# Final norm moved inside the last down pass, and a re-ordered middle stage

## The reference

```
h = h + mlstm(rmsnorm(h)) ; h = h + swiglu(rmsnorm(h))           # layer 0 ("front", then FFN 0)
k, v = split(rmsnorm(h) @ w_kv)      ; k = rope(k)               # shared keys and values, 4 heads
q    = rope(rmsnorm(h) @ w_q)                                    # 16 query heads
o    = softmax([q k_meta | q k_window | sink]) @ [v_meta | v_window]   # window of 128, chunks of 64
h = h + o @ w_o                                                  # "middle stage"
h = h + swiglu(rmsnorm(h))                                       # layer 1 (FFN 1)
y = h * rsqrt(mean(h*h) + eps) * g_final                         # final norm
rope(x) = [x1 cos - x2 sin, x2 cos + x1 sin]
swiglu(x) = (silu(x w_g) * (x w_u)) @ w_down
```

## Time and profile before

| | |
|---|---|
| median of 3 runs | 2649.29 us |
| the profiled execution's own time | 2651.17 us |
| its span (first to last instruction) | 2649.4 us |
| mean granted TensorE clock | 0.992 of full speed |
| PE busy | 2587.5 us (98%) |
| DVE busy | 1097.2 us (41%) |
| ACT busy | 682.6 us (26%) |
| POOL busy | 628.9 us (24%) |
| DMA | 174.43 MB, 66 GB/s over the span |

### The profile page before, as it was taken

One profiled execution on the slowest core, in us unless ns is written; L12 is line 12 of the kernel. 1 busy time (PEld: TensorE's weight loads), 2 busy tenths in 40 slices (PEclk: granted clock), 3 DMA queues, 4 the chain that ended last, 5 costly groups with the idle time before them and its releaser, 6 DMA issues. The chain is left out here.

```text
span 2649.4 us, 37939 instructions
## 1 busy us (share of the span) xinstructions
PE 2587.5 (98%) x15350; PEld 2520.1 (95%) x15350; DVE 1097.2 (41%) x2306; ACT 682.6 (26%) x1513; POOL 628.9 (24%) x626
## 2 busy tenths in 40 slices
PE   8999999999999999999998998999999999999997
PEld 7989999999999999999997987899999999999997
DVE  6444455154322323333246555655233232223335
ACT  5222333042111111111125555434111111111112
POOL 2222213212122111121226232225112212211211
PEclk9999999999999999999999999999999999999999
DMA  4445564101111111111112136011111111111112
GB/s 146 147 123 155 159 176 147 57 25 56 32 48 40 41 48 40 40 40 40 48 51 50 43 79 160 17 33 48 40 40 41 48 33 48 48 41 41 40 40 80
DMA packets 251153, 174.43 MB, mean 66 GB/s; under 512 B 54392, under 2 KB 240940, under 8 KB 250948
## 3 DMA queue, kind: packets, MB, share of 16 engines
q1 hardware_dynamic: 250788, 171.96, 22.5%
q10 hardware_dynamic: 192, 0.04, 0.0%
HBM read 138.57 MB, written 35.20 MB: 66 GB/s over the span
## 5 line engine op out<-in xcount | busy, mean ns | idle before, releaser
L193 POOL TENSOR_TENSOR wl<-raw,wh 128x512 fp32r<-128x512 f32 x264 | 337.7, 1303 | 1291.8 <-ACT wh L185 1291.8
L345 PE MATMUL psum<-xh,wl 128*128 128x400 f32 (+1 forms) x1872 | 430.2, 338 | 0.0
L345 PE MATMUL psum<-xl,wh 128*128 128x400 f32 (+1 forms) x1872 | 428.5, 337 | 0.0
L345 PE MATMUL psum<-xh,wh 128*128 128x400 f32 (+1 forms) x1872 | 427.4, 336 | 0.0
L471 DVE TENSOR_TENSOR h<-h,psum 128x384 f32<-128x384 f32 (+1 forms) x528 | 265.1, 553 | 280.5 <-PE psum L365 267.1
L345 PEld LDWEIGHTS psum<-xh,wl 128*128 128x128 f32 x1872 | 336.8, 188 | 0.0
L345 PEld LDWEIGHTS psum<-xl,wh 128*128 128x128 f32 x1872 | 336.6, 188 | 0.0
L345 PEld LDWEIGHTS psum<-xh,wh 128*128 128x128 f32 x1872 | 335.9, 188 | 0.0
L2023 PE MATMUL psum<-xh,wh 128*128 128x384 f32 (+1 forms) x792 | 275.7, 348 | 5.5 <-DVE xl L2173 2.7
L2023 PE MATMUL psum<-xl,wh 128*128 128x384 f32 (+1 forms) x792 | 271.4, 343 | 0.0
L2023 PE MATMUL psum<-xh,wl 128*128 128x384 f32 (+1 forms) x792 | 270.0, 341 | 0.0
(11 more groups left out here) (249 smaller groups left out, 3687.2 us busy)
## 6 DMA issues: line engine op xcount, KB each, us to landing
raw<-in_w_gate_up SPq DMA_DIRECT2D x88, 512.0 KB, 3.8
raw<-in_w_down SPq DMA_DIRECT2D x44, 512.0 KB, 3.6
raw<-in_a_w_in SPq DMA_DIRECT2D x24, 512.0 KB, 4.7
fr_qkv<-qkv_d SPq DMA_DIRECT2D x36, 256.0 KB, 3.8
qkv_d<-fr_tmp SPq DMA_DIRECT2D x32, 192.0 KB, 2.0
hn_d<-fr_hn_turned SPq DMA_DIRECT2D x36, 128.0 KB, 3.3
fr_xin<-in_x_prompt SPq DMA_DIRECT2D x8, 512.0 KB, 5.2
fr_decode_state<-in_state_c SPq DMA_DIRECT2D x4, 1024.0 KB, 7.2
```

The lines of the kernel that those rows point to most:

```text
L193: pool.tensor_tensor(wl[:, self.slot(p), v], raw[:, self.raw_of(p), v], wh[:, self.slot(p), v].bitcast(F32), ALU.subtract).then_inc(self.w ...
L345: y = pe.matmul(psum[:, bank + c, 0:nt], w[:, k, :], x[:, k, t0:t0 + nt], start=(k == 0 and m == 0), stop=(k == KD - 1 and m == 2))
```

## The change

Final norm:

- Block `final` is gone; a class `Final` works inside the one block. ACT squares each tile of `h` as DVE adds it, POOL sums them, for each token piece. In the down pass, `between` puts PE work behind the tiles m = 2 to 7 of pieces 1 and 2: at m = 2 the token sums of the piece before (three matmuls of one column), and at each of m = 2 to 7 four transposes of it (`turn`). DVE scales the turned tiles between its adds (`after`). The third piece is turned and scaled behind the pass. Stores are halves of 256 KB, 18 of them.

Middle stage:

- `swap(g)` waits for the group itself, no longer for the cosine product, and the cosine product waits for the swap.
- Squares have four buffers, not two; on the way in, root 0 stands ahead of the split of piece 2, five of the squares of piece 2 ahead of swap(0), the low halves of weight tile 2 ahead of the sums of piece 2; the low halves of piece 2's activations come behind group 0 on DVE; total 1 moves from behind g = 0 to behind g = 1, total 2 from behind g = 3 to behind g = 4.
- The second pair's tiles are loaded one by one (`KV_LOAD`, `Q_LOAD`) from g = 25 on; the query tile (n = 11, c = 0) after g = 35, (n = 11, c = 1) after g = 36, piece 2 after g = 38 to 42; the cached values after g = 46 instead of 38.
- Output chunks are split tile by tile, after g = 34, 38 and 42; PE waits for each tile of 128 features.
- The second pair's steps have slots 37, 39, 41, 43, 44, 45, 47 ... 61, where they had 37, 38, 39, 41, 42, 43, 45 ... 60.

```diff
-FIRST0, FIRST1, SPREAD1 = 16, 37, 25
+FIRST0, FIRST1 = 16, 37
+KV_LOAD = {25: 0, 31: 1, 42: 2}
+Q_LOAD = {26: (0, 0), 28: (0, 1), 29: (1, 0), 30: (1, 1), 32: (2, 0), 33: (2, 1), 35: (3, 0), 36: (3, 1),
+          38: (0, 2), 39: (1, 2), 40: (2, 2), 41: (3, 2)}
-OG_SPLIT = {34: 0, 35: 1, 40: 2}
+OG_SPLIT = {34: 0, 38: 1, 42: 2}
...
-            slot = FIRST0 + z if z < NSTEP else FIRST1 + ((z - NSTEP) * SPREAD1) // NSTEP
+            i = z % NSTEP
+            slot = FIRST0 + z if z < NSTEP else FIRST1 + (2 * i if i < 4 else 6 + (4 * (i - 3)) // 3)
...                                                                      # SP
-            if 33 <= g < 36:
-                c = g - 33
+            if g in KV_LOAD:
+                c = KV_LOAD[g]
-                sp.wait_ge(self.tst[c], 16 * 6)
+                sp.wait_ge(self.tst[c], 16 * 2)
...
+            if g in Q_LOAD:
+                m, c = Q_LOAD[g]
+                sp.wait_ge(self.tst[c], 16 * (3 + m))
+                sp.wait_ge(self.sc, 6 * c + 6)
...                                                                      # POOL
+        self.weight_lo(pool, 2)
         sums(2)
-        self.weight_lo(pool, 2)
...                                                                      # ACT, swap(g)
-            act.wait_ge(self.rope, 2 * self.ropes(g) - 1)
-            act.wait_ge(self.evac, g)
+            k = self.ropes(g)
+            act.wait_ge(self.done, g + 1)
+            if k > 1:
+                act.wait_ge(self.evac, self.roped(k - 1) + 1)
...                                                                      # PE
-            if g == 0:
+            if g == 1:
                 total(1)
-            if g == 3:
+            if g == 4:
                 total(2)
...                                                                      # DVE, leave(g)
             else:
+                dve.wait_ge(self.swapped, self.ropes(g))
                 dve.tensor_tensor(self.stg[:, t0:t0 + nt], psum[:, self.bank(g), 0:nt], self.cosr[:, t0:t0 + nt], ALU.mult).then_inc(self.rope, 1)
...                                                                      # class Final
+    def between(self, pe, c, m):
+
+        if c and m == 2:
+            self.totals(pe, c - 1)
+        if c and m >= 2:
+            self.turn(pe, 6 * (c - 1) + m - 2)
...
+    def after(self, dve, q):
+
+        c, m = q // 8, q % 8
+        if c and m == 2:
+            self.means(dve, c - 1)
+        if c and m >= 3:
+            self.normal(dve, 6 * (c - 1) + m - 3)
+        if c == 2 and m == 0:
+            self.normal(dve, 5)
```

More of the change, by code:

```diff
@@ L312, in scalar, with tensor @@
         hidden_hi(self.n_hidden - 1)
-    def tensor(self, pe, bank_free):
+    def tensor(self, pe, bank_free, between=None):
         s, tok = self.s, self.tok
@@ L390, in down @@
                     z.then_inc(self.dn_done, 1)
+                    if between is not None:
+                        between(pe, c, m)
         totals_after = (0, 3, 6) if self.early else (3, 5, 7)
@@ L628, in ropes, with roped @@
         return sum(1 for x in self.groups[:g + 1] if x[0] % 6 != 1)
+    def roped(self, k):
+        return [g for g, x in enumerate(self.groups[:self.NPROJ]) if x[0] % 6 != 1][k - 1]
     def q_places(self, c, m):
@@ L809, in sync @@
                     .then_inc(self.kvl[c], 16)
[L810 to L814, removed]
+            if g in Q_LOAD:
+                m, c = Q_LOAD[g]
+                sp.wait_ge(self.tst[c], 16 * (3 + m))
+                sp.wait_ge(self.sc, 6 * c + 6)
+                for i, dst, src in self.q_places(c, m):
+                    v = self.kvq_d[2 + m, :, src:src + dst.shape[1] * dst.shape[2]]
+                    sp.dma_start(dst, v.rearrange("p (i t) -> p i t", i=dst.shape[1])).then_inc(self.kvl[c], 16)
+            if g == 46:
                 sp.wait_ge(self.row_st[2], 16 * 4 * NB)
@@ L907, in x_split, with squares @@
                 act.activation(self.xh[:, k, t0:t0 + nt], self.h[:, k, t0:t0 + nt], ACT.Copy).then_inc(self.x_hi, 1)
-        def squares(c):
+        def squares(c, first=0, end=KD):
             t0, nt = TOK_ALL[c]
-            for k in range(KD):
+            for k in range(first, end):
                 n = 7 * c + k - 1
-                if k and n >= 2:
-                    act.wait_ge(self.x_sum, self.z["x_sum"] + n - 1)
-                dst = self.sq[:, n % 2, 0:nt] if k else self.acc[:, t0:t0 + nt]
+                if k and n >= 4:
+                    act.wait_ge(self.x_sum, self.z["x_sum"] + n - 3)
+                dst = self.sq[:, n % 4, 0:nt] if k else self.acc[:, t0:t0 + nt]
                 act.activation(dst, self.h[:, k, t0:t0 + nt], ACT.Square).then_inc(self.x_sq, 1)
@@ L971, in chunk_hi @@
             act.wait_ge(self.og_ld[c], 16)
-            act.activation(self.xh[:, 0:4, t0:t0 + nt], self.xl[:, 0:4, t0:t0 + nt].bitcast(F32), ACT.Copy).then_inc(self.chi, 1)
+            for k in range(4):
+                act.activation(self.xh[:, k, t0:t0 + nt], self.xl[:, k, t0:t0 + nt].bitcast(F32), ACT.Copy).then_inc(self.chi, 1)
         self.weight_hi(act, 0)
@@ L979, in scalar @@
         self.weight_hi(act, 1)
+        root(0)
         x_split(2)
-        root(0)
-        root(1)
         self.weight_hi(act, 2)
+        squares(2, 0, 5)
         for g in range(self.NG):
@@ L1000, in scalar @@
             if g == 0:
-                squares(2)
-            if g == 3:
-                root(2)
+                squares(2, 5, KD)
             if g in self.at_value and self.at_value[g] >= NSTEP:
@@ L1057, in out @@
             pe.wait_ge(self.evac, g - 2)
-            if half == 0:
-                pe.wait_ge(self.clo, c + 1)
-            else:
+            if half:
                 pe.wait_ge(self.slo, (6, 12, 18)[c])
@@ L1065, in out @@
             for k in range(4):
+                if half == 0:
+                    pe.wait_ge(self.clo, 4 * c + k + 1)
                 for m, (y, x) in enumerate(((hi, self.xh), (hi, self.xl), (lo, self.xh))):
@@ L1264, in leave_rope @@
                 dst = self.kv[:, 0, t0:t0 + nt] if n == 0 else x
[L1265 removed]
+                dve.tensor_tensor(dst, x, swp, ALU.add).then_inc(self.evac, 1)
                 return
@@ L1317, in chunk_lo @@
             t0, nt = TOK_REAL[c]
-            x = self.xl[:, 0:4, t0:t0 + nt]
-            dve.wait_ge(self.chi, c + 1)
-            dve.tensor_tensor(x, x.bitcast(F32), self.xh[:, 0:4, t0:t0 + nt].bitcast(F32), ALU.subtract).then_inc(self.clo, 1)
+            for k in range(4):
+                x = self.xl[:, k, t0:t0 + nt]
+                dve.wait_ge(self.chi, 4 * c + k + 1)
+                dve.tensor_tensor(x, x.bitcast(F32), self.xh[:, k, t0:t0 + nt].bitcast(F32), ALU.subtract).then_inc(self.clo, 1)
         def turned(z):
@@ L1355, in denominators @@
             dve.reciprocal(self.st[:, u, 7, :], self.st[:, u, 6, :]).then_inc(self.rdn, 1)
-        for k in range(KD):
-            self.x_low(dve, 2, k)
         tables(0)
@@ L1372, in vector @@
             if g == 0:
+                for k in range(KD):
+                    self.x_low(dve, 2, k)
                 tables(1)
@@ L1716, in _ @@
             m.sync(sp)
+            fin.sync(sp)
             f1.sync(sp)
+            fin.store(sp)
             m.finished(sp)
@@ L2139, in _ @@
             m.tensor(pe)
-            f1.tensor(pe, m.bank_free)
+            f1.tensor(pe, m.bank_free, fin.between)
+            fin.tensor(pe)
         @block.vector
@@ L2485 @@
+            f1.vector(dve, fin.after)
+            fin.vector(dve)
 OUTS = [("y_p", (1, SEQ, D)), ("y_s", (NB, TS, D)),
```

187 lines of the change are left out of this document (113 added, 74 removed).

## The result

The changed kernel takes 2655.2 us (median of 17 runs, 2649.98 to 2657.5), the kernel before 2648.62 in the same comparison (17 runs): ratio 1.0022, 95% interval 1.0015 to 1.0029, so 0.2% slower, 5.8 us. The forecast was 2639, 10 faster, with a range of 2622 to 2652, so the direction was missed too. The profiled execution took 2655.61 us with a span of 2653.6.

The account below looks back on a forecast made before the run. PE, busy 98% of the span, bounds the kernel, so time comes from its stands, halved clock, work or tail. Terms -9.5 + 21.3 - 14.8 - 7.6 = -10.6 take the median from 2649.29 to 2638.7, forecast 2639, range 2622 to 2652.

Parts of the forecast that it names:

- C: Groups 36 to 42: the stands of 3.64 and 7.57 and their half clock go, about 1 remains; -14.8 us.
- D: The end: final norm inside the down pass lengthens it by 7.4 and shortens the tail behind it; -7.6 us.
- A: Way into the middle stage: PE's stands and half clock in groups 0 to 5 go, part given back; -9.5 us.
- B: Attention part: the cosine product's added wait for the swap makes PE stand, 19.3 plus 2.0 of half clock; +21.3 us.
- the 12.7: Groups 0 to 5: us lost against full speed, 9.9 of stands and the rest half clock; all to go.
- A, given back: Behind the way in, late evictions at the cached turns: 2.8 wait and 1.5 half clock, less 1.1 at another stand.
- Rival 1: Attention part: PE reaches the transposes later, so the added wait does not show, B 0 to 5; 2618 to 2623; 11%.
- Rival 2: Attention part: each of B's fourteen stands of 1 to 2.5 us sets the clock back; 2660 us; 8%.
- Rival 4: Last down pass: the clock falls to half in the last 16 tiles, where the transposes are; 2656 us; 2%.
- Rival 3: Late evictions and query load: A gives -5 for -9.5, C -9 for -14.8; 2649 us, no change; 18%.

Follow-up runs that it names:

- the better DVE order: Changed kernel, but in projection groups of DVE's list the rows copy and the step's output stand ahead of the cosine product; 2626.95 us.

## Why the prediction was wrong

- **The sum.** Its net was -10.6 out of terms of 8 to 21, and the trace has +4.2. All four terms have their sign, and C and D about their size. Of the 14.8 missing, 7.2 is A, 5.7 is B, 1.4 is C and 1.4 D, less the 0.9 of untouched code. The direction failed by A and B together: with either as forecast the net would have been a gain, but of 3.0 or 1.5 and not of 10.
- **A is the step that failed**, and in it the claim on the low halves: "the last at 1425.3, where PE needs it from 1421 on, one by one, so it is just ahead". PE was there at 1419.2, since group 0 began at 1401.15 where I had left it at 1402.59. The first low half was begun at 1419.43 and done at 1420.8, and the last was done at 1428.2. The price was misread. The 1.02 of the earlier trace rows, which I called the price beside POOL's sums, is a mean over eight in which POOL's last sum ended at 1409.3: one took 1.03, then 1.62, 1.63 and 2.25 beside weight halves and a scaling, and four took 0.55 with POOL idle. Here is one of them, from the trace of before:

```profile
1409.66 1.62 DVE L1201 TENSOR_TENSOR xl<-h,xh 128x384 fp32r<-128x384 f32 x1
```

  In place of the forecast's five at 0.95 and three at 0.5 there were four at 1.35, one at 2.25 and three at 0.55. The kernel with squares added on 16 columns shows POOL's additions as the cause of the four. (The rule that I weighed there and set aside, of the Trainium skill, "GPSIMD Engine Reference", 1. Specifications, on interfaces shared by GpSimd and VectorE, agrees with these numbers: 8.77 with POOL's additions beside, 5.58 without most of them.) Four stands of 1.7, 0.4, 0.5 and 0.85 went with a halved clock, 0.66 over 10 us, up to another 3.4. So groups 0 to 5 took 34.2 and not 28.3, and 5.9 of the 12.7 was missing.
- **A, given back.** This was right in kind and too small, 5.1 for 3.2: 3.1 at the cached turn (2.1 more than before) for my 2.8, 1.7 of half clock for 1.5, but the stand at the first score grew from 1.3 to 2.0 where I had it shrink by 1.1. The chain of evictions that I priced from fast rows was slower beside POOL: DVE's scalings with the sines and cosines took 1.5 to 2.2 us beside POOL's weight halves. And mending the low halves mends only a part: with them in DVE's idle time 6.7 was given back, and the whole kernel gained 2.4. Alone, with B, and with the better DVE order A is worth nothing (+0.8, -0.3, +0.3 us against the same without it, each within its interval).
- **B, its mechanism, was right to the instruction**: fourteen stands, eight of 1.03 to 1.11 for 1.05, 1.54 at group 34 for 1.3, 2.13 and 2.23 at the rows copy for 2.0 and 1.9, 2.18 and 2.70 for 2.15 and 2.5, nothing at 21 to 23. They sum to 21.0 for 19.3. The term that was mis-sized is the half clock behind them: 2.0 forecast, four drops of 1.7 measured, 6.7. Group 19's stand was 1.64 for 1.05, since its swap waited for the eviction before it.
- **C** was right: -13.4 for -14.8. The load of the query tile was not late, and no wait over 0.4 is left there in the changed kernel. With earlier groups the window copies on POOL cost 1.5 to 2.0 at the first score of the second pair, in the kernels where the wait of B is missing or harmless.
- **D** was right in the pass (+7.0 for +7.4) and 1.8 short behind it: POOL's last sum ended 2.2 behind the last matmul, the last scaling ended 8.5 behind it for my 7.4, and from there to the end it was 4.2 for my 3.5.
- **The rivals.** Rival 1 was wrong. Rival 2's place and price were right for four of the stands of 1.6 and more and wrong for the short ones: the 24 us window with three of them has 1.00. Rival 4 didn't happen: the clock is 1.00 from 2621 to 2641, and the tile's period in the pass rose only by what the transposes take (adds of DVE 1.51 us apart, before 1.04). Rival 3 came half true: A gave little, partly by the late evictions that it names, and C gave what it should.
- **The range** had B at 10 to 25 and A at -4 to -13. Both measured values lie just outside, on the same side. Both hold half clock that I had put too low: none in groups 0 to 5, where it took up to 3.4, and 2.0 in B, where it took 6.7.

## What to carry to other kernels

A wait costs what is queued behind it on its engine. Before paying for one, reorder: putting the rows copy and the step's output ahead of the waiting one was worth 26 us here, with the wait kept. When a gap on the critical engine is closed by moving work on another, read that work at the price of its new neighbour, not its old one; here the low halves were moved to stand beside POOL's sums, and groups 0 to 5 took 34.2 us in place of 28.6. That price has to be read from single instructions: a merged row of eight had 1.02 as its mean and nothing near it but one. Closing the first gap also moved the wait on: DVE's late evictions gave half or more of the gain back. And a stand of PE of 1.6 to 3.1 us may cost 1.7 us of clock besides; of the seven single ones in the changed kernel's middle stage behind 1440 five did.

## What the runs showed of the hardware

- Beside POOL, DVE slowed only where both its inputs are in SBUF, and by what POOL did. A low half of 128x384 took 0.55 alone, 1.34 to 1.37 beside POOL's additions of 128x384, 1.6 beside its low halves of a weight and 2.25 beside its scaling of a raw tile; beside additions of 16 columns it took 0.57. In the changed kernel, while POOL makes a weight's low halves (1442.86 to 1445.4) and scales a raw tile (to 1447.2), the cosine product with one input in PSUM keeps its time, and the sine product has four times that:

```profile
1444.97 0.57 DVE L1268 TENSOR_TENSOR mid_staged<-psum,mid_cos 128x400 f32<-128x400 f32 x1 [1.80 <-ACT mid_swapped L948]
1445.46 2.23 DVE L1277 TENSOR_TENSOR mid_swapped<-mid_swapped,mid_sin 128x400 f32<-128x400 f32 x1
```

- The length of a stand alone does not decide on the clock: 1.64 at 1512 was followed by 0.72 for 6 us, 2.18 at 1622 and 1.98 at 1492 by 1.00. Even one and the same stand goes both ways. At the first score PE stands for 2.01 in the kernel with the better DVE order, and the clock behind it (1489.3 to 1492.5) is 0.50; in the kernel with the low halves in DVE's idle time it stands for 2.00, and the clock (1489 to 1493) is 1.00. What decides is left open.
- Four transposes between down tiles added 0.47 us to a tile, at a clock of 1.00. Transposes alone did not lower it either: in the final norm of the kernel before PE did nothing else from 2625.9 to 2639.1, 10.2 us of them, at 1.00.
